# A two-layer diffusion backbone on one core: the last layer's attention is cut into a part over all keys but the context's last tile and a part over that tile

## What is computed

```python
# neighbourhood attention, 4 heads of 64, and windowed GQA with sink logits, 8 query heads on 2 key heads
s_ctx = einsum(q, kc) * scale                       # kc, vc: keys and values of the CONTEXT tokens
probs = softmax(concat([s_own + bias, s_ctx, (s_sink)]))
y     = probs_own @ v + probs_ctx @ vc
mix   = merge_branches(y_a, y_b, y_c, y_d, gates) @ w_o
x     = layer_norm(alpha * x + g1 * mix)
ffn   = peer_ffn(...)    # per token: 8 heads x 16 experts = 128 rows of (u, v) gathered from 16,384
x     = layer_norm(alpha * x + g2 * ffn)
```

## Time and profile before

| | |
|---|---|
| median of 3 runs | 3086.38 us (3084.62 to 3088.89) |
| the profiled execution | 3092.83 us |
| its span, first to last instruction | 3090.9 us |
| mean granted TensorE clock | 0.782 of 2.4 GHz |
| PE busy | 2398.1 us (78%) |
| DVE busy | 1922.8 us (62%) |
| ACT busy | 411.1 us (13%) |
| POOL busy | 730.6 us (24%) |
| chain that ended last, by engine | PE 46%, DMA 24%, DVE 17%, POOL 5%, issue 5%, ACT 3% |

### The profile page before, as it was taken

One profiled execution on the slowest core, in us unless ns is written; L12 is line 12 of the kernel. 1 busy time (PEld: TensorE's weight loads), 2 busy tenths in 40 slices (PEclk: granted clock), 3 DMA queues, 4 the chain that ended last, 5 costly groups with the idle time before them and its releaser, 6 DMA issues.

```text
span 3090.9 us, 34672 instructions
## 1 busy us (share of the span) xinstructions
PE 2398.1 (78%) x11936; PEld 1286.7 (42%) x11936; DVE 1922.8 (62%) x6218; ACT 411.1 (13%) x1018; POOL 730.6 (24%) x779
## 2 busy tenths in 40 slices
PE   7989995878999778577989977666897557675655
PEld 6778891434655434124545541113785011121111
DVE  3879977876454557857754455554558855555554
ACT  2141120133000201012110010000421000000000
POOL 0000002222222222332322223331001323333332
PEclk8999996888999889568989985666998555655556
DMA  8628748998999978878999999998144989999997
GB/s 324 239 105 327 281 162 352 362 356 325 420 408 393 372 308 354 341 293 356 401 395 420 398 379 404 390 393 339 52 143 179 351 331 393 401 388 404 393 393 301
DMA packets 155376, 1029.87 MB, mean 333 GB/s; under 512 B 19136, under 2 KB 29888, under 8 KB 34496
## 3 DMA queue, kind: packets, MB, share of 16 engines
q0 software_dynamic: 110592, 805.36, 65.4%
q1 hardware_dynamic: 31648, 209.70, 17.4%
q10 hardware_dynamic: 12960, 12.59, 1.2%
HBM read 1018.66 MB, written 8.91 MB: 332 GB/s over the span
## 4 chain that ended last, share of the span: by engine, by line
PE 46%; DMA 24%; DVE 17%; POOL 5%; issue 5%; ACT 3%; ACTq 0%; DVEq 0%; SPq 0%; POOLq 0%
DMA ring<-in_peer_uv,eT 22%; PE PS L1255 12%; DVE ring L2290 8%; PE PS L902 7%; PE PS L1274 5%; POOL ring L720 5%; PE PS L1013 4%; PE PS L824 3%; PE PS L923 2%; PE PS L986 2%; PE PS L1095 2%; PE PS L943 2%; PE PS L1192 1%; PE PS L826 1%; PE PS L787 1%
## 5 line engine op out<-in xcount | busy, mean ns | idle before, releaser
L2290 DVE CUSTOM_DVE_ANT_0 ring<-ring,PS 128x512 f32<-128x512 f32 x1536 | 994.2, 685 | 830.8 <-PE PS L1274 453.8
L720 POOL DMA_INDIRECT ring<-in_peer_uv,eT x768 | 728.7, 949 | 2331.2 <-PE PS L1255 1450.5
L1274 PE MATMUL PS<-xr,onesb 3*128 3x512 bf16 x1536 | 554.0, 489 | 483.0 <-DVE hcol L2290 394.2
L1255 PE MATMUL PS<-ring,zcol 128*32 128x512 f32 x3072 | 579.1, 893 | 99.3 <-DVE zcol L2300 97.2
L1274 PEld LDWEIGHTS PS<-xr,onesb 3*128 3x128 bf16 x1536 | 107.8, 95 | 1057.5 <-DVE hcol L2290 554.2
L1255 PEld LDWEIGHTS PS<-ring,zcol 128*32 128x32 f32 x3072 | 102.8, 142 | 383.7 <-issue 216.2
L902 PE MATMUL PS<-uT,W 128*128 128x256 f32 x1024 | 248.7, 392 | 0.0
L1658 ACT ACTIVATE ge<-hdot 128x4 f32<-128x4 f32 x192 | 39.4, 205 | 1409.5 <-DVE hdot L2295 1380.4
L902 PEld LDWEIGHTS PS<-uT,W 128*128 128x128 f32 x1024 | 193.3, 194 | 49.1 <-issue 22.8
L1731 DVE CUSTOM_DVE_ANT_0 ring<-ring 128x1024 f32<-128x1024 f32 x160 | 190.1, 1221 | 7.6 <-DMA ring<-in_w_rows 3.5
L824 PE MATMUL PS<-uT,W 128*128 128x256 f32 (+1 forms) x672 | 156.7, 387 | 8.5 <-ACT uT L1338 8.1
(11 more groups left out here) (296 smaller groups left out, 2185.7 us busy)
## 6 DMA issues: line engine op xcount, KB each, us to landing
ring<-in_w_rows SPq DMA_DIRECT2D x40, 1024.0 KB, 8.1
W<-in_w_in SPq DMA_DIRECT2D x30, 1024.0 KB
W<-in_w_gate SPq DMA_DIRECT2D x16, 1408.0 KB
W<-in_w_gate SPq DMA_DIRECT2D x16, 1280.0 KB
W<-in_w_out SPq DMA_DIRECT2D x20, 1024.0 KB
W<-in_w_gate SPq DMA_DIRECT2D x16, 1152.0 KB
ring<-in_w_q SPq DMA_DIRECT2D x16, 1024.0 KB, 13.4
ring<-in_peer_uv,eT POOLq DMA_INDIRECT x768
```

Of the source, the lines that this page charges most:

```text
L720: pool.indirect_dma_start(ring[:, slot, :], None, (peer_uv0, peer_uv1)[b.l], bass.IndirectOffsetOnAxis(eT[:, f % 2, t:t + 1], 0)).then_inc ...
L1255: last = T.matmul(PS[k * NR:(k + 1) * NR, (6 + h) * 512:(7 + h) * 512], zcol[:, g % 2, k, NR - 1 - at:2 * NR - 1 - at], ring[:, slot, D + ...
L1274: T.matmul(bank(x_bank(q, n) + h), onesb[p0:p0 + 3, :], xr[p0:p0 + 3, g % 2, h * 512:(h + 1) * 512], start=True, stop=True)\
L2290: V.tensor_tensor_reduce(out=u_half, in0=u_half, in1=bank(x_bank(q, n) + h), scale=1.0, scalar=0.0, op0=ALU.mult, op1=ALU.add, accum_out=h ...
```

## The change

A new part, `("part", BL1)`, stands behind `front KV1A`, ahead of `after 1, 1, 0`. It does the twelve jobs over three tiles of keys (the two latent tiles and the context's first): scores, mask and maximum, exponential with the row sum, transposes by the identity, values, and leaves for each job the unnormalised sum in `yb`, the maxima in `MA` and the sums in `SA`. Each job has six steps of kind `part` at 1.2 tokens, so the 72 steps take 86 of the context's second 128 tokens, from token 154 to 240.

In `back BL1` the twelve-job pipeline is gone. `attend` does the context's second tile for all twelve jobs in three groups of four: 24 scores of 128 columns, maxima over 512 columns at once, the new maximum against the old one (and the sink), a factor `AL` for the old sums, 24 exponentials of 128 columns, one scaling of 1,024 and one of 512 columns per group, 24 transposes, and a product that adds the first part (by the identity) to the values of the last tile in PSUM. All steps of kind `job` still stand behind it, with no tokens ready then. In the diff below, `part_` is TensorE's; the three functions `attend` are TensorE's, ScalarE's and VectorE's, in this order, and `late_exps(g)` is the buffer of a group's eight exponentials, `group_out(g)` the 512 columns of `yb` that hold its outputs.

```diff
-          ("after", 1, 0, SLACK), ("residual", CTX0, 0), ("norm", KV1A), ("front", KV1A),
+          ("after", 1, 0, SLACK), ("residual", CTX0, 0), ("norm", KV1A), ("front", KV1A), ("part", BL1),
           ("after", 1, 1, 0), ("residual", CTX0, 1),
...
-         "late": 2.4}
+         "late": 2.4, "part": 1.2}
...
+            def part_(b):
+                a = at_of["part", b]
+                for n, (br, c, qt) in enumerate(JOBS):
+                    of_q = (nq, gqk)[br]
+                    if n:
+                        pe.wait_ge(a["psm"], a.at("psm", n))
+                    for e, r_ in enumerate(halves()):
+                        q_ = of_q[r_, c, qt * P:(qt + 1) * P]
+                        own, ctx_ = (nkb_l[r_, c, :], nkb_c[r_, c, 0:P]) if br == 0 else (gqk[r_, 4, :], gkc[r_, 0:P])
+                        T.matmul(bank(2 + e, 0, TOK), q_, own, start=True, stop=True)
+                        last = T.matmul(bank(2 + e, TOK, TOK + P), q_, ctx_, start=True, stop=True)
+                    last.then_inc(a["pS"], 1)
+                    yield "part"
+                    yield "part"
+                    yield "part"
+                    pe.wait_ge(a["pexp"], a.at("pexp", n + 1))
...
+                            last = T.transpose(bank(4 + e, q * P, (q + 1) * P), exA[:, e, q * P:(q + 1) * P], ident[:, :])
+                    last.then_inc(a["pptp"], 1)
+                    yield "part"
+                    yield "part"
+                    pe.wait_ge(a["ppts"], a.at("ppts", n + 1))
...
+                            last = T.matmul(bank(4 + e, 3 * P, 3 * P + DH), PT[:, (e * 3 + q) * P:(e * 3 + q + 1) * P], v_,
+                                            start=(q == 0), stop=(q == 2))
+                    last.then_inc(a["pO"], 1)
+                    yield "part"
...
+            def attend(a):
+                def scores(g):
+                    for n in range(4 * g, 4 * g + 4):
+                        br, c, qt = JOBS[n]
+                        for e, r_ in enumerate(halves()):
+                            at = n % 4 * P
+                            k_ = nkb_c[r_, c, P:TOK] if br == 0 else gkc[r_, P:TOK]
+                            last = T.matmul(bank(2 + 2 * g + e, at, at + P), (nq, gqk)[br][r_, c, qt * P:(qt + 1) * P], k_,
+                                            start=True, stop=True)
+                    last.then_inc(a["S"], 1)
+                def transposed(g):
+                    pe.wait_ge(a["pn"], a.at("pn", g + 1))
+                    for m in range(8):
+                        last = T.transpose(bank(2 + 2 * g + m // 4, m % 4 * P, (m % 4 + 1) * P), late_exps(g)[:, m, :], ident[:, :])
+                    last.then_inc(a["ptp"], 1)
+                def values(g):
+                    pe.wait_ge(a["pts"], a.at("pts", g + 1))
+                    if g == 2:
+                        pe.wait_ge(a["y"], a.at("y", 1))
+                    for m in range(4):
+                        n = 4 * g + m
+                        br, c, qt = JOBS[n]
+                        T.matmul(bank(g % 2, m * P, (m + 1) * P), first_part(n), ident[:, :], start=True, stop=False)
+                        for e in range(2):
+                            v_ = nvf_c[:, 1, (2 * c + e) * DH:(2 * c + e + 1) * DH] if br == 0 else gvb_c[:, 1, e * DH:(e + 1) * DH]
+                            last = T.matmul(PS[e * DH:(e + 1) * DH, g % 2 * 512 + m * P:g % 2 * 512 + (m + 1) * P], v_,
+                                            late_exps(g)[:, 2 * m + e, :], start=False, stop=True)
+                    last.then_inc(a["O"], 1)
+                for g in range(GROUPS):
+                    scores(g)
+                transposed(0)
+                transposed(1)
+                values(0)
+                transposed(2)
+                values(1)
+                values(2)
...
+            def attend(a):
+                def exps(g):
+                    c0 = 8 * g
+                    act.wait_ge(a["sm"], a.at("sm", g + 1))
+                    A(AL[:, c0:c0 + 8], DA[:, c0:c0 + 8], ACT.Exp)
+                    if g:
+                        A(SK[:, c0:c0 + 8], DS[:, c0:c0 + 8], ACT.Exp)
+                    for m in range(8):
+                        last = A(late_exps(g)[:, m, :], bank(2 + 2 * g + m % 2, m // 2 * P, (m // 2 + 1) * P), ACT.Exp,
+                                 bias=NM[:, c0 + m:c0 + m + 1], accum_out=SB[:, c0 + m:c0 + m + 1])
+                    last.then_inc(a["exp"], 1)
+                def probs(g):
+                    act.wait_ge(a["ptp"], a.at("ptp", g + 1))
+                    for h in range(2):
+                        last = A(late_exps(g)[:, 4 * h:4 * h + 4, :].rearrange("p m k -> p (m k)"), bank(2 + 2 * g + h), ACT.Copy)
+                    last.then_inc(a["pts"], 1)
+                def outputs(g):
+                    act.wait_ge(a["O"], a.at("O", g + 1))
+                    A(group_out(g), bank(g % 2), ACT.Copy).then_inc(a["y"], 1)
+                exps(0)
+                exps(1)
+                probs(0)
+                exps(2)
+                probs(1)
+                outputs(0)
+                probs(2)
+                outputs(1)
+                outputs(2)
...
+            def attend(a):
+                def bounded(g):
+                    of = slice(8 * g, 8 * g + 8)
+                    dve.wait_ge(a["S"], a.at("S", g + 1))
+                    for e in range(2):
+                        ch.add(V.reduce_max(MB[:, 8 * g + e:8 * g + 8:2],
+                                            bank(2 + 2 * g + e).rearrange("p (m k) -> p m k", m=4), AX))
+                    ch.wait()
+                    ch.link(V.tensor_tensor(MB[:, of], MB[:, of], MA[:, of], ALU.max))
+                    if g:
+                        heads = sink[:, :].rearrange("p (e c) -> p c e", e=2)[:, 2 * g - 2:2 * g, :].unsqueeze(2).to_broadcast([P, 2, 2, 2])
+                        as4 = lambda t: t[:, of].rearrange("p (c q e) -> p c q e", c=2, q=2)
+                        ch.link(V.tensor_tensor(as4(MB), as4(MB), heads, ALU.max))
+                        ch.add(V.tensor_tensor(as4(DS), heads, as4(MB), ALU.subtract))
+                    ch.add(V.tensor_scalar(NM[:, of], MB[:, of], -1.0, None, ALU.mult))
+                    V.tensor_tensor(DA[:, of], MA[:, of], MB[:, of], ALU.subtract).then_inc(a["sm"], 1)
+                def normed(g):
+                    of = slice(8 * g, 8 * g + 8)
+                    dve.wait_ge(a["exp"], a.at("exp", g + 1))
+                    ch.link(V.tensor_tensor(CA[:, of], AL[:, of], SA[:, of], ALU.mult))
+                    ch.link(V.tensor_tensor(CR[:, of], CA[:, of], SB[:, of], ALU.add))
+                    if g:
+                        ch.link(V.tensor_tensor(CR[:, of], CR[:, of], SK[:, of], ALU.add))
+                    ch.link(V.reciprocal(CR[:, of], CR[:, of]))
+                    ch.link(V.tensor_tensor(CA[:, of], AL[:, of], CR[:, of], ALU.mult))
+                    ch.add(V.tensor_tensor(late_exps(g), late_exps(g), CR[:, of].unsqueeze(2).to_broadcast([P, 8, P]), ALU.mult))
+                    parts_ = group_out(g).rearrange("p (m d) -> p m d", m=8)
+                    V.tensor_tensor(parts_, parts_, CA[:, of].unsqueeze(2).to_broadcast([P, 8, DH]), ALU.mult).then_inc(a["pn"], 1)
+                bounded(0)
+                bounded(1)
+                normed(0)
+                bounded(2)
+                normed(1)
+                normed(2)
```

More of the change, by code:

```diff
@@ L731, in experts @@
                     yield
-            weave.run(dict(ada=ada, norm=norm, front=front, early=early, back=back, residual=residual), experts(), ask_ahead)
+            weave.run(dict(ada=ada, norm=norm, front=front, early=early, part=part_, back=back, residual=residual), experts(), ask_ahead)
         @block.tensor
@@ L1115, in back @@
                 begun = []
-                scores(0)
-                for n in range(len(JOBS) + 3):
+                if b.early:
+                    yield from attend(a)
+                else:
+                    scores(0)
+                for n in range(0 if b.early else len(JOBS) + 3):
                     if s == 0 and n + 1 < len(JOBS):
@@ L1291, in _ @@
             woven["pe"] = Weave()
-            woven["pe"].run(dict(ada=ada, norm=norm, front=front, early=early, back=back, residual=residual), experts())
+            woven["pe"].run(dict(ada=ada, norm=norm, front=front, early=early, part=part_, back=back, residual=residual), experts())
         @block.scalar
@@ L1673, in _ @@
             woven["act"] = Weave()
-            woven["act"].run(dict(ada=ada, norm=norm, front=front, early=early, back=back, residual=residual), experts())
+            woven["act"].run(dict(ada=ada, norm=norm, front=front, early=early, part=part_, back=back, residual=residual), experts())
         @block.vector
```

97 lines of the change are left out of this document (91 added, 6 removed).

## The result

The changed kernel takes 3069.89 us (median of 16 runs, 3062.43 to 3083.92) beside 3088.36 us (16 runs, 3082.79 to 3092.39) for the kernel before: a ratio of 0.9943, with a 95% interval of 0.9934 to 0.9952. That is 17.6 us less (0.0057 x 3088). The profiled execution took 3070.98 us, at the same mean granted clock, 0.782.

A forecast was written before the change was run, and what follows sets the result against it. The DMA engines alone were taken to bound the context's last tokens, while the attention ran uncovered for 61.1 us. 61.1 - 32 - 6 = 23 us less takes the median from 3086.4 to 3063.3 us, range 3052 to 3078.

The forecast's parts named there:

- The removed stage: The attention running alone, from its first score to the merge's first matmul: 61.1 us, removed in full.
- So I take 4 of the possible 9 us: 32.: New attention stage: 4 us added for TensorE's pieces partly at low clock, giving 32 us, between 28 and 37.
- the sum of pieces, 28: New attention stage: its chain of pieces at full clock, 27.1 us, with some ten handovers at 0.1, 28 us.
- the clock rival: The new attention runs at 1.2 GHz, 37 us, and the merge begins so: 15 us less, 3071; chance 0.12.
- There jobs stood closer and convolution taps ran too, so I take 6 us for the twelve.: Expert stream: the twelve added jobs lengthen it by 6 us, between 0 and 13; layer 0's jobs cost 1.1 each.
- 3.4, or 6.8 at 1.2 GHz: Stream, TensorE's work per job in us: scores 1.05, six transposes 1.45, six values at most 0.9.
- 5.4 us of added work against 5.3 us of waits per job: Stream: TensorE's 3.4 plus VectorE's 2.0 us at full clock just fit into VectorE's waits for gathers.
- the stream starves its gathers: Rival: jobs hold back token spreading and weighing, slots are asked for late; 13 to 20 us cost, 3070 to 3078; chance 0.17.
- All of `part` is hidden: Rival: the jobs cost the stream nothing and the clock holds; 33 us less, 3053; chance 0.14.
- Slower: Rival: at 1.2 GHz nothing overlaps, 42 us more against 29 saved, 3099; decides at 2.4 us per job; chance 0.05.
- The table loads: Stream: a load of 1.28 us ahead of a group's gelu, twelve times, costs nothing while ScalarE is early.
- What would show it: Signs: gathers 2.7 to 2.8 us, DMA share 0.95 or more, stage 28 to 37 us, exponentials about 0.4, merge unchanged.

The follow-up runs named there:

- alone: The changed kernel with its first part moved out of the expert stream, behind the second front and straight ahead of the last attention; 3174.53 us in one execution.
- no_tables: The changed kernel with the first part's 24 exponentials replaced by identity copies with the row sum, so no table is switched in the stream; 3070.46 us, ratio 0.9939.
- ahead_again: Repeat of the changed kernel with a job every eight tokens, its scores and transposes between a group's last token and the weighing; 3058.83 us, ratio 0.9894.
- after_again: The changed kernel itself measured once more, nothing edited; 3071.07 us, ratio 0.9935 to the kernel before.
- Experiment 3: The changed kernel rerun beside three with a job every eight tokens, pieces at different places in the group of four; 3058.54 to 3074.36 us.
- ahead: The changed kernel with a job every eight tokens, scores and transposes ahead of the weighing (3058.16, repeated 3058.83 us) or of a group's last token (3058.54 us).
- light_dve: The changed kernel with VectorE's four reductions of a job left out from the second job on; 3058.39 us, ratio 0.9893.

## Why the prediction was right, and which terms were off

The forecast was 3063.3 us, 23 less than before; measured are 3069.9 and 17.6 less, inside its range. (2 us of the difference in the time come from the kernel before, whose median was 3086.4 over 3 runs and 3088.4 over 16.) The mechanism is the one forecast: the stage of 61.1 us leaves, a short one comes, and the rest is paid in the stream. Two terms were mis-sized, in opposite directions.

**The removed stage.** Right in full: first score to merge was 61.07 us and is 28.31.

**"So I take 4 of the possible 9 us: 32."** The stage took 28.3. That is the sum of pieces, 28, but it comes about in part by luck. Exponentials 0.34 apart instead of 0.39 and two copies of 512 columns in 1.1 were quicker, and a maximum over 512 columns (0.65) was as assumed. Each of the two last products, taken at 2.0, took 3.1 or 3.2 (2200.59 to 2203.71 and 2203.64 to 2206.86 us, at a clock of 1.00), and the end of the stage is TensorE's, not `normed(2)`. And the pieces were not all "at full clock": the eight transposes of 1.94 us ran at a granted clock of 0.50 in the kernel before (2148.4 to 2150.5 us), so what the prediction doubled for its bound was the slow price already; the changed kernel shows 1.97 at 0.50 and 1.09 at 1.00. The clock's 4 us did not come: the mean was 0.82, and slow pieces lay partly beside ScalarE's exponentials. Other profiles size it: the same stage took 30.4 us at a mean of 0.67 in *alone*, and 31.0 at 0.72 in both *no_tables* and *ahead_again*, 2 to 3 more. So the possible 9 us was too high a bound, and the clock rival with its 37 us was wrong, while the forecast's 32 was near what the stage takes in some executions. By the Trainium skill ("TensorE: Matmul & The Clock Gate", "What's actually happening"), where activity releases the throttle, the direction is right: the clock had risen to 1.00 when the merge began.

**"There jobs stood closer and convolution taps ran too, so I take 6 us for the twelve."** It is 12.7 in the profile of after, 14.8 in *after_again* (289.6 - 274.8): at the upper end of the stated bounds, or just past it. The size of the job on TensorE was not what failed. "3.4, or 6.8 at 1.2 GHz" measures 3.35 us at a clock of 1.00 and 6.0 at 0.50 (*alone*), though by two errors that cancel: six values took 1.55 at 1.00 and not "at most 0.9", and six transposes 0.87 and not 1.45, which again came from the earlier trace rows, at 0.50. What failed is that the argument set averages against each other: 5.4 us of added work against 5.3 us of waits per job. It asked how much room VectorE and TensorE have, and not where in a group of four tokens the room is. Experiment 3 shows that this place decides it: no cost to within a us ahead of the weighing, 20 us straight behind it, with the same work. At 7.2 tokens per job the pieces of the changed kernel fall at all places in turn, and its cost lies between. The 6 us themselves came from another stretch, with other work in it; that they were within a factor of three is luck as much as reading. Both numbers of the stream without a job in it, 274.8 before and 273.9 in *alone*, are what these are measured against.

**Of the rivals,** "the stream starves its gathers" came true in kind, at its low price: the pieces hold back the spreading, the weighing comes late, slots are asked for late; DMA share 0.97. "All of `part` is hidden" is what the *ahead* kernels do. "Slower" needed 2.4 us per job; it was 1.06. That *alone* is 87 us slower shows how much of the change hangs on its cover.

**The table loads** were rightly left at nothing, or 3 us by *no_tables*. The rule of the Trainium skill ("ScalarE: Activation LUTs", "What ACT_TABLE_LOAD costs") of a drain beside the load is not borne out: at 2183.68 us again the exponential began as the load ended, and the gelus' delay is 0.28 us per group, with 0.27 before.

**What would show it:** of these signs, a DMA share over 0.95, the stage between 28 and 37 us, exponentials at 0.4 us and the length from the merge to the first weighing of `LAT1` (149.9 us against 149.2) held. The gathers took 221 / 78 = 2.83 us each, a little over the 2.7 to 2.8 named.

What stays open: why *light_dve* gains more in its time than in its stream; what the missing full clock alone would give in the stream, which no run tried; and how the 12.7 us divide between TensorE's and VectorE's pieces, since taking away either lets the other run unseen.

## What to carry to other kernels

Work that is woven into a stream bound by transfers is to be priced by its place in the stream's cycle, not by the mean slack of its engines: ahead of the step that releases the slots, while the engine waits anyway, it was free; straight behind the longest piece, where the next consumer already waits, more than half of the time that it added there was lost. If the weave has a rate, make the period a whole number of cycles and try the phases, which takes an edit of two lines. When the price of a piece is read from a trace, read the granted clock of its stretch beside it. And before moving a chain of small dependent steps, price it alone: here its own length was 120.8 us, and only the cover made it worth splitting.

## What the runs showed of the hardware

The granted clock did not follow the busy share alone. In *alone*, TensorE was 60% busy for 110 us (65.47 of 110) in pieces of 1.5 and 4.5 us with pauses of one and three us between, and the clock stayed at 0.50 throughout. The attention before, 83% busy (50.90 of 61) with pauses of at most 1.5 us, was granted 0.97; the new stage, 63% busy (17.60 of 28), 0.82; the stream with the jobs, 80% busy (176.24 of 221), 0.65. In the new stage TensorE paused for 7.25 us behind the scores; the clock was 1.00 from 2183 to 2187 us, 0.50 from 2188 to 2197 and 1.00 again from 2198 on. That the low clock made the difference between the 8 us per job that I expected of *alone* and the 10 measured is likely (a job's pieces took 6.0 us there and 3.35 at a clock of 1.00) but was not tried apart.

Matmuls with 128 columns of weights and 64 of data did not come at half the price of those with 128 of data: in *alone*, at a clock of 0.50, the twelve records of six values took 2.83 us, 0.24 each, and six transposes of 128 columns 1.54 us, 0.26 each; at a clock of 1.00 in the changed kernel it was 1.55 us and 0.87, 0.13 and 0.15 each.
